# Softmax weights turned by a product with a diagonal of the reciprocal sums

## The reference, cut to what matters

```python
def causal_softmax_attention(q, k, v, scale):
    ...
    def block(qb, start):
        s = jnp.einsum('bhqd,bhkd->bhqk', qb, k).astype(jnp.float32) * scale
        qpos = start + jnp.arange(Q_BLOCK, dtype=jnp.int32)
        s = jnp.where(kpos[None, :] <= qpos[:, None], s, neg)
        p = jax.nn.softmax(s, axis=-1)
        return jnp.einsum('bhqk,bhkd->bhqd', p.astype(v.dtype), v)
```

## Time and profile before

| | before |
|---|---|
| median of 3 runs | 2439.66 us (2438.17 to 2441.11) |
| profiled execution, its own time | 2441.37 us |
| its span in the trace | 2439.6 us |
| TensorE busy | 2364.3 us, 97% |
| VectorE busy | 1379.0 us, 57% |
| ScalarE busy | 980.8 us, 40% |
| GpSimd busy | 241.9 us, 10% |
| mean granted TensorE clock | 0.989 |

### The profile page before, as it was taken

The page is one execution under the profiler, slowest core; times in us unless marked ns, Lnnn a source line. Parts: engine busy times, 40 slices in busy tenths (PEclk is TensorE's granted clock), DMA queues, the critical chain, the costliest instruction groups (busy, mean ns, idle before and its releaser), DMA issues.

```text
span 2439.6 us, 35763 instructions
## 1 busy us (share of the span) xinstructions
PE 2364.3 (97%) x13448; PEld 1887.9 (77%) x13448; DVE 1379.0 (57%) x1936; ACT 980.8 (40%) x1507; POOL 241.9 (10%) x192
## 2 busy tenths in 40 slices
PE   8999999999999999999999999999999999999998
PEld 6765777888887765777888887777888888788887
DVE  4557867666545447857656545675443445533443
ACT  5535435323235535535323244564332233422332
POOL 0041210000022032301000002101000001000001
PEclk9999999999999999999999998999999999999999
DMA  4210014656432211003656521222222232222322
GB/s 158 81 61 24 19 49 143 192 195 193 144 103 78 87 61 35 19 29 122 197 190 195 167 95 60 87 86 93 98 95 95 95 97 76 78 95 96 100 97 86
DMA packets 68796, 248.33 MB, mean 102 GB/s; under 512 B 7632, under 2 KB 8144, under 8 KB 68688
## 3 DMA queue, kind: packets, MB, share of 16 engines
q1 hardware_dynamic: 68688, 246.85, 30.8%
HBM read 244.72 MB, written 2.10 MB: 101 GB/s over the span
## 4 chain that ended last, share of the span: by engine, by line
PE 85%; DVE 7%; ACT 4%; issue 2%; DMA 0%; POOL 0%; SPq 0%; DVEq 0%; ACTq 0%
PE dense L588 24%; PE dense L590 24%; PE dense L589 24%; PE aux L695 2%; PE aux L882 1%; ACT wh L1352 1%; PE aux L852 1%; DVE wl L1966 1%; PE aux L869 1%; PE aux L960 1%; PE aux L971 1%; PE aux L1056 1%; PE aux L856 1%; PE dense L616 1%; PE aux L702 0%
## 5 line engine op out<-in xcount | busy, mean ns | idle before, releaser
L588 PE MATMUL dense<-xh,wh 128*128 128x512 f32 x1840 | 734.0, 399 | 25.4 <-DVE wl L1966 10.7
L1352 ACT ACTIVATE wh<-raw 128x1024 fp32r<-128x1024 f32 x346 | 366.7, 1060 | 944.0 <-PE dense L590 936.8
L1966 DVE TENSOR_TENSOR wl<-raw,wh 128x1024 fp32r<-128x1024 f32 x346 | 427.1, 1235 | 535.4 <-ACT wh L1352 533.9
L590 PE MATMUL dense<-xh,wl 128*128 128x512 f32 x1840 | 718.3, 390 | 0.0
L589 PE MATMUL dense<-xl,wh 128*128 128x512 f32 x1840 | 718.2, 390 | 0.0
L588 PEld LDWEIGHTS dense<-xh,wh 128*128 128x128 f32 x1840 | 346.6, 188 | 122.2 <-issue 28.0
L590 PEld LDWEIGHTS dense<-xh,wl 128*128 128x128 f32 x1840 | 346.4, 188 | 73.5
L589 PEld LDWEIGHTS dense<-xl,wh 128*128 128x128 f32 x1840 | 346.7, 188 | 73.0 <-issue 4.1
L588 PE MATMUL dense<-hidh,wh 128*128 128x512 f32 x928 | 363.5, 392 | 4.9 <-DVE hidl L1998 2.1
L589 PE MATMUL dense<-hidl,wh 128*128 128x512 f32 x928 | 361.9, 390 | 0.0
L590 PE MATMUL dense<-hidh,wl 128*128 128x512 f32 x928 | 361.7, 390 | 0.0
(11 more groups left out here) (386 smaller groups left out, 2432.6 us busy)
## 6 DMA issues: line engine op xcount, KB each, us to landing
raw<-stream SPq DMA_DIRECT2D x362, 512.0 KB, 3.4
mraw<-mod_stream SPq DMA_DIRECT2D x96, 512.0 KB, 4.2
x<-x_t SPq DMA_DIRECT2D x4, 512.0 KB, 7.2
y_t<-x SPq DMA_DIRECT2D x8, 256.0 KB, 2.0
cst<-consts SPq DMA_DIRECT2D x1, 993.0 KB, 9.3
band<-bands SPq DMA_DIRECT2D x1, 576.0 KB, 4.6
cond<-c_rows SPq DMA_DIRECT2D x1, 512.0 KB, 10.5
pv_next<-vecs SPq DMA_DIRECT2D x3, 82.5 KB, 4.6
```

Of the source, the lines that this page charges most:

```text
L588: pe.matmul(o, a, h, start=first, stop=False)
L590: return pe.matmul(o, b, h, start=False, stop=last)
L1352: act.activation(wh[:, slot].rearrange("p k m -> p (k m)"), raw[:, slot, :], ACT.Copy).then_inc(hi_done, 1)
L1966: tt(wl[:, slot].rearrange("p k m -> p (k m)"), raw[:, slot, :], wh[:, slot].rearrange("p k m -> p (k m)").bitcast(F32), SUB)\
```

## The change

The mla units no longer scale `keep` on VectorE. VectorE only forms the reciprocal sums and signals `rsum_ready`. ScalarE writes a 128x128 matrix into the first 128 columns of `wts`: the identity with each row times the reciprocal sum of that row, which is a diagonal matrix. It does so in its loop body u after `weights(u + 1)` and ahead of the extra work and `turned(u)`. TensorE's `turn(u)` then multiplies: for each of the i + 1 blocks an fp32 matmul with the block of `keep` as the stationary operand and the diagonal as the moving one, in place of the transpose with the identity. Its result is the transposed and scaled block. Since `keep` is now read by TensorE, ScalarE's `weights(u)` for mla units waits for `t_ready` of unit u - 2 in place of `w_ready`, and VectorE no longer waits for `t_ready`.

```diff
                     for j in range(i + 1):
-                        m = pe.transpose(aux[2][:, j * P:(j + 1) * P],
-                                         wts[:, u % 2, j * P:(j + 1) * P], const("ident"))
+                        if UNITS[u][0] == "sb":
+                            m = pe.transpose(aux[2][:, j * P:(j + 1) * P],
+                                             wts[:, u % 2, j * P:(j + 1) * P], const("ident"))
+                        else:
+                            m = pe.matmul(aux[2][:, j * P:(j + 1) * P],
+                                          keep[:, u % 2, j * P:(j + 1) * P],
+                                          wts[:, u % 2, 0:P], start=True, stop=True)
                     m.then_inc(t_ready, 1)
...
                     if u >= 2:
-                        act.wait_ge(w_ready, L * NU + u - 1)
+                        act.wait_ge(w_ready if kind == "sb" else t_ready, L * NU + u - 1)
...
+                def scaled(u):
+
+                    if UNITS[u][0] == "mla":
+                        act.wait_ge(rsum_ready, L * (NU // 2) + u - NU // 2 + 1)
+                        act.activation(wts[:, u % 2, 0:P], const("ident"), ACT.Copy,
+                                       scale=small[:, 13, u % 2:u % 2 + 1]).then_inc(w_ready, 1)
...
                     if u + 1 < NU:
                         weights(u + 1)
+                    scaled(u)
...
-                    if u >= 2:
+                    if u >= 2 and kind == "sb":
                         dve.wait_ge(t_ready, L * NU + u - 1)
...
                     else:
-                        chain(dve.reciprocal(small[:, 13, b:b + 1], small[:, 3, b:b + 1]))
-                        ts(wts[:, b, 0:n], keep[:, b, 0:n], small[:, 13, b:b + 1], None, MUL)\
-                            .then_inc(w_ready, 1)
+                        dve.reciprocal(small[:, 13, b:b + 1], small[:, 3, b:b + 1])\
+                            .then_inc(rsum_ready, 1)
```

More of the change, by code:

```diff
@@ L428, in build @@
         krot_ready, kh_rope = sem("krot_ready"), sem("kh_rope")
+        rsum_ready = sem("rsum_ready")
         z_ready, w_act, mx_ready, w_ready = (sem("z_ready"), sem("w_act"), sem("mx_ready"),
```

## The result

The changed kernel takes 2463.85 us (median of 4 runs, 2462.91 to 2465.97), against 2440.36 us before (4 runs). The ratio is 1.0092 (95% interval 1.0079 to 1.0105), so 22.4 us slower (0.0092 x 2440.36). The forecast was 2456.5 us with a range to 2467.

The account below looks back on a forecast made before the run. Bound by TensorE's work, the VectorE-to-TensorE hand-over and, in the second half, VectorE's queue. Work 6.0 plus waits 2.4 makes 8.4 us a layer, 16.8 in both: 2456.5 us, own range 2452.5 to 2461, wide 2447 to 2467.

Parts of the forecast that it names:

- TensorE's work: In the mla turns, a matmul for each transpose costs 0.15 us more a block, 6.0 us a layer.
- The alternative of 0.44 us a block: Rival: the product in the mla turns takes four records a block, 13.2 us a layer, 2471 us in all; 4%.
- The new instruction and the hand-over: ScalarE's diagonal takes 0.37 us and, standing behind weights(u + 1), starts unit 16's turn 0.5 us later.
- The waits: TensorE before mla turns: 3.6 us more in units 16 to 23, 1.1 less in 24 to 31, 2.4 a layer.
- the sign that I had named: In the new trace, waits before the last eight mla turns should be shorter than before.
- The clock: In both mla stretches, the same low-clock loss as before, about 4.5 us for 17 us of low clock.
- a sign of being wrong: The prediction is wrong if the clock's low stretches differ much from 17 us.
- VectorE's relief: In mla units VectorE has 6.5 us less a layer, worth something only in the second half, where it sets the pace.
- The rival: Clock falls earlier or longer, in units 18 to 23 too: 3.5 us more a layer, 2463.5 us; 17%.
- the wide range: Whole kernel: 2447 to 2467 us, leaving out less than 2 in 10, over the clock cases and a cheap product.
- the clock rival: Low clock in units 18 to 23 as well, 3.5 us more a layer, 2463.5 us; 17%.
- the forecast's own range: Whole kernel: 2452.5 to 2461 us, from 0.11 or 0.15 us a block and 0.1 us on ScalarE's instruction; 48%.

Follow-up runs that it names:

- with fillers: One idle fp32 128x512 matmul added before the weights wait in turns of units 16, 18 and 26; changed kernel +11.2 us, kernel before -3.9 us, against before.
- the product alone: Kernel before with only the mla transposes replaced by fp32 matmuls with the identity, VectorE still scaling; +5.1 us against the kernel before.
- the hand-over alone: Changed kernel with TensorE transposing keep by the identity, diagonal made but not multiplied in; +14.4 us against the kernel before, +4.9 us with idle matmuls.
- diagonal-first run: Changed kernel with VectorE's reciprocal ahead of row_max(u + 1) and ScalarE's diagonal ahead of weights(u + 1); +2.0 us against the kernel before.
- scaling-first run: Kernel before with VectorE's reciprocal and scaling ahead of row_max(u + 1) in mla units; -0.5 us against the kernel before.
- scaling first, with fillers: Kernel before with VectorE's reciprocal and scaling ahead of row_max(u + 1), plus idle matmuls in units 16, 18 and 26; -4.4 us against the kernel before.

## Why the prediction was right, and where its sizes were off

**TensorE's work.** Said: 0.15 us more a block, 6.0 a layer. Measured: a turn of four blocks holds TensorE 1.04 us (222.83 to 223.87), before 0.53 (188.30 for the turn, its successor at 188.83): 0.13 a block. A turn of one block went from 0.21 (200.45 to 200.66) to 0.37 us (229.42 to 229.79). Over a layer that is 4 x (0.16 + 0.32 + 0.44 + 0.51), the differences for one to four blocks, or 5.7 us. Right. The alternative of 0.44 us a block is out.

**The new instruction and the hand-over.** Said: 0.37 us and 0.5 us later at unit 16. Measured: 0.39 and 0.47 (0.80 - 0.33). Right. That it is the place that costs and not the length, the two runs with the diagonal ahead of the exponential show.

**The waits.** Said: 3.6 us more in units 16 to 23 and 1.1 us less after them, with units 17, 19, 20 and 21 waiting 0.4, 0.4, 0.9 and 1.1. Measured in the rows of layer 0: 5.5 us against 3.3 in units 16 to 23, and 3.3 against 2.1 in units 24 to 31. So the last eight turns wait longer in these two traces, and the sign that I had named, shorter waits there, did not show. Units 19, 20 and 21 wait 0.23, 0.75 and 0.96, and unit 17 doesn't wait. The rows count from the end of the matmul before and not from TensorE's issue point, and in both kernels they fall partly into low clock, so the clean test is the stretch at full clock. The kernel before and the changed kernel, both with fillers, turns of units 24, 26, 27, 30 and 31 of layer 0:

```profile
221.28 0.28 PE L873 MATMUL aux<-cst,wts 128*128 128x128 f32 x1
...
226.35 0.44 PE L873 MATMUL aux<-cst,wts 128*128 128x128 f32 x2 [0.20 <-DVE wts L2189]
...
228.54 0.44 PE L873 MATMUL aux<-cst,wts 128*128 128x128 f32 x2 [0.49 <-DVE wts L2189]
...
235.59 0.66 PE L873 MATMUL aux<-cst,wts 128*128 128x128 f32 x4 [1.11 <-DVE wts L2189]
```

```profile
227.19 0.43 PE L878 MATMUL aux<-wts,keep 128*128 128x128 f32 x2
...
233.51 0.71 PE L878 MATMUL aux<-wts,keep 128*128 128x128 f32 x4 [0.70 <-ACT wts L1551]
...
235.54 0.71 PE L878 MATMUL aux<-wts,keep 128*128 128x128 f32 x4
...
242.68 1.16 PE L878 MATMUL aux<-wts,keep 128*128 128x128 f32 x8 [0.74 <-ACT wts L1551]
...
244.81 1.16 PE L878 MATMUL aux<-wts,keep 128*128 128x128 f32 x8 [0.18 <-ACT wts L1551]
```

To the turn of unit 24 it is 24.99 us before (221.28 - 196.29) and 30.79 after (227.19 - 196.40), 5.8 more; from there to the end of the stretch it is 18.47 and 20.49, 2.0 more. With 2.9 us of product work in each half, the waits grew by 2.9 in the first (said 3.6) and shrank by 0.9 in the second (said 1.1). The mechanism was right, at full clock. In all it is 51.28 - 43.45 = 7.8 us a layer for work and waits together, where 8.4 was said.

The parts alone are 46.80 - 43.45 = 3.4 us for the hand-over (said 3.8) and 46.0 - 43.45 = 2.6 us for the product (said 3.5; without fillers, but at full clock). They add to 5.9, not to 7.8. About 1.5 of the missing 1.9 lie in the last eight units, where the product alone takes 0.8 us more, the hand-over alone 0.2 less and both together 2.0 more. That the product alone hides there in waits for VectorE, which the hand-over takes away, fits this; no run shows it by itself.

**The clock.** This is the term that was mis-sized. Said as the likeliest: the same loss as before, 4.5 us, so nothing in the difference. By the stretches with and without fillers the loss was (44.50 - 43.46) + (45.79 - 43.45) = 3.4 us before and (54.96 - 51.28) + (56.26 - 51.28) = 8.7 us after, 5.3 us more. Two things were wrong. The low clock did not keep its duration: 24 us in place of 17, which the prediction had named as a sign of being wrong. And its price did not stay the same either. The prediction had two that don't agree, 0.4 us per us from the difference of the layers, and 4.5 us for 17, which is 0.26. Measured are 3.4 us for 17, or 0.20, in the kernel before, 8.7 us for 24, or 0.36, in the changed one, and for the hand-over alone 8.2 us for 24, or 0.34. At the old price the 7 us more would have cost 1.4 us and not 5.3.

The rows show where the price comes from. In the kernel before, the turns of units 27 and 30 of layer 0:

```profile
228.47 0.69 PE L869 MATMUL aux<-cst,wts 128*128 128x128 f32 x2
...
236.55 0.66 PE L869 MATMUL aux<-cst,wts 128*128 128x128 f32 x4 [0.25 <-DVE wts L2185]
```

With the clock up these turns waited 0.49 and 1.11 us for VectorE's scaling; with the low clock from 227.2 to 234.0 us nothing and 0.25. So 1.35 us of the slower TensorE fell into waits that were there anyway, and the stretch lost 1.04. The changed kernel has no such waits: unit 27 doesn't wait and unit 30 waits 0.74 us, with low clock and without. There 6.8 us of low clock made the way from unit 26's turn to unit 31's 2.6 us longer (235.74 to 249.62, against 233.51 to 244.81). VectorE's relief made the low clock dearer.

The rival said that the clock would fall in units 16 to 23 as well, for 3.5 us more a layer and 2463.5 us in all. It did fall there: to the turn of unit 24 the changed kernel takes 1.1 us more in layer 0 and 2.1 in layer 1 without fillers than with them, the kernel before no more. That is 3.2 us of the 5.3. The other 2.1 are the dearer low clock in units 24 to 31, which neither the forecast nor the rival had. The rival had 17%, though I had named the longer waits that speak for it.

**The sum.** 2 x 7.8 = 15.7 us at full clock and 5.3 us of clock make the 20.9 of the two stretches. The remaining 1.5 us up to 22.4 are in neither term; single executions differ by as much. Said were 16.8 us, and nothing for the clock. The measured 2463.85 us lies in the wide range only because that range was drawn over the clock rival; it is above the forecast's own range of 2452.5 to 2461, and the terms named for that range give 2450.9 to 2458.9. That 2463.85 is so near the rival's 2463.5 is partly luck: its 7 us of clock were 5.3, the rest 1.1 us less than said, and 1.5 us came from elsewhere.

**The other side.** VectorE's relief came through nowhere as a gain over the kernel before, not even in the diagonal-first run, whose 45.15 us a stretch stands against 43.45 with fillers. Against the product alone (46.0) it is 0.9 us a layer less, but that run also keeps VectorE's order, and the order by itself gave some 0.7 us in the kernel before at full clock (42.78 against 43.45), so little is left for the relief.

The Trainium skill ("TensorE: Matmul & The Clock Gate", Part 4) has transposes not counting as busy for the clock. The product-alone run agrees in its direction (clock 1.00 with products, 0.92 and 0.89 with transposes, same waits), but it also has more work between the same waits. Other readings speak against it: the earlier trace rows have transposes alone at 1.00, layer 0 of the scaling-first run has transposes, no fillers, waits of 1.08, 1.30 and 1.26 us and clock 1.00, and the changed kernel, with products, had as much low clock in its stretches as the hand-over alone, with transposes: 23.9 us each. Whether the kind of matmul matters beyond its time stays open.

## What to carry to other kernels

An instruction given to an engine with room costs what stands ahead of it in that engine's queue: here 0.39 us of ScalarE, 16 times a layer, behind the next unit's exponential was worth 12 us at full clock and 20 us with what it did to the clock; with ScalarE and VectorE both reordered, only +2.0 us was left of the change. Ask of a change that adds waits on TensorE what it does to the granted clock, above all where the profile already shows a fall behind waits of the same length: every us of low clock cost 0.2 us in the kernel before, where TensorE had waits for VectorE to make it up in, and 0.36 us in the changed one, where it had not. A change that takes such waits away makes the low clock dearer. Where such waits can't be removed, an idle matmul that fits into them may pay for itself (-3.9 us from six of them), and it is a good probe for what the clock takes.

## What the runs showed of the hardware

- Six idle fp32 matmuls of about 1.1 us each took 11.2 us off the changed kernel and 3.9 us off the kernel before. I had expected 5 and 4.5 at the most.
- The same code had a low-clock stretch of 3.4 us at about 109 us in some profiled executions (the changed kernel, the hand-over alone, the scaling first; with fillers, the hand-over alone at 107 us) and none in others, before any difference in the code is reached. A span compared between two single executions carries a few us of this.
- At clock 1.00 the two layers' stretches agree within 0.01 us in four kernels (the three with fillers above and the diagonal first); in two others they differ by 0.13 us (the product alone) and 0.23 us (scaling first, with fillers). The 1.3 us between the layers in the traces of before and after went away with the low clock.
- The same low clock has no fixed price: 6.8 us of it, from the turn of unit 26 of layer 0 on, cost the kernel before 1.0 us and the changed kernel 2.6.
